# The second norm's shift and scale of layer one: from split weight tiles on TensorE to a weighted sum on VectorE

## What is computed

```python
mod = jax.nn.silu(c) @ w_mod[l] + b_mod[l]                  # latent tokens; the same with c_ctx for context
sh1, sc1, gt1, sh2, sc2, gt2 = jnp.split(mod[:, None, :], 6, axis=-1)
...
y = (g_a * y_a + g_b * y_b + g_c * y_c) @ w_out
x = x + gt1 * y
x = x + gt2 * swiglu(rms_norm(x, g_norm2) * (1 + sc2) + sh2, w_ffn_in, w_ffn_out)
```

## Time and profile before

| | us |
|---|---|
| median of three runs | 2443.31 |
| time of the profiled execution | 2441.43 |
| its span, first to last instruction | 2439.6 |
| TensorE busy | 2357.4 (97%) |
| VectorE busy | 1340.9 (55%) |
| ScalarE busy | 1046.8 (43%) |
| GpSimd busy | 735.0 (30%) |

### The profile page before, as it was taken

How to read it: one execution, slowest core, us unless ns; L and a number is a source line. 1 busy time by engine, 2 the same in 40 slices (tenths; PEclk the granted TensorE clock), 3 DMA queues, 4 the chain that set the end, 5 groups by cost and what they waited for, 6 DMA issues and landing times.

```text
span 2439.6 us, 33714 instructions
## 1 busy us (share of the span) xinstructions
PE 2357.4 (97%) x13224; PEld 2126.8 (87%) x13224; DVE 1340.9 (55%) x2079; ACT 1046.8 (43%) x2079; POOL 735.0 (30%) x545
## 2 busy tenths in 40 slices
PE   7999999989989999999999999999999999999999
PEld 3888999989989989999999997777878887888887
DVE  5666677699953444454443436767888954211111
ACT  4666667642253342212221227666764253422222
POOL 2211112100064524343333333112220054444443
PEclk9999999999999999999999999999999999999999
DMA  6100111022233414433343322111112323233333
GB/s 253 45 22 28 39 35 44 25 94 83 70 100 104 143 44 130 130 112 119 120 134 109 117 77 78 36 35 41 47 38 84 104 87 129 87 100 94 101 95 95
DMA packets 130828, 209.01 MB, mean 86 GB/s; under 512 B 12784, under 2 KB 58096, under 8 KB 130544
## 3 DMA queue, kind: packets, MB, share of 16 engines
q1 hardware_dynamic: 130672, 206.86, 26.7%
HBM read 202.62 MB, written 4.19 MB: 85 GB/s over the span
## 4 chain that ended last, share of the span: by engine, by line
PE 54%; DVE 5%; ACT 3%; issue 1%; DVEq 0%; ACTq 0%
PE acc L648 15%; PE acc L650 15%; PE acc L649 15%; PE aux L648 2%; PE aux L649 2%; PE aux L650 2%; DVE RB L1629 2%; ACT M L1093 1%; PE sco L832 1%; DVE M L1629 1%; PE aux L845 1%; DVE NM L1672 1%; PE sco L800 1%; ACT RB L1093 1%; ACT R L1093 1%
## 5 line engine op out<-in xcount | busy, mean ns | idle before, releaser
L564 POOL TENSOR_TENSOR WLO<-STG,WHI 128x512 fp32r<-128x512 f32 (+2 forms) x532 | 728.1, 1390 | 1687.0 <-ACT WHI L1089 1686.8
L648 PE MATMUL acc<-H,WHI 128*128 128x384 f32 (+2 forms) x1976 | 710.9, 360 | 14.7 <-DVE H L1885 8.6
L650 PE MATMUL acc<-H,WLO 128*128 128x384 f32 (+2 forms) x1976 | 695.6, 352 | 0.0
L649 PE MATMUL acc<-H,WHI 128*128 128x384 f32 (+2 forms) x1976 | 695.5, 352 | 0.0
L1089 ACT ACTIVATE WHI<-STG 128x512 fp32r<-128x512 f32 (+2 forms) x648 | 348.9, 586 | 409.8 <-PE acc L650 362.1
L648 PEld LDWEIGHTS acc<-H,WHI 128*128 128x128 f32 x1976 | 374.5, 190 | 43.6 <-issue 14.0
L650 PEld LDWEIGHTS acc<-H,WLO 128*128 128x128 f32 x1976 | 374.0, 189 | 25.4
L649 PEld LDWEIGHTS acc<-H,WHI 128*128 128x128 f32 x1976 | 374.7, 190 | 24.0
L648 PE MATMUL acc<-RB,WHI 128*128 128x384 f32 (+1 forms) x816 | 288.6, 354 | 3.2 <-DVE RB L1629 1.4
L1629 DVE TENSOR_TENSOR T<-G,acc 128x384 f32<-128x384 f32 (+1 forms) x101 | 60.3, 597 | 413.7 <-PE acc L650 305.7
L650 PE MATMUL acc<-RB,WLO 128*128 128x384 f32 (+1 forms) x816 | 287.6, 352 | 0.0
(11 more groups left out here) (144 smaller groups left out, 2942.9 us busy)
## 6 DMA issues: line engine op xcount, KB each, us to landing
STG<-in_w_fi SPq DMA_DIRECT2D x176, 256.0 KB, 2.7
M<-in_w_mod SPq DMA_DIRECT2D x56, 512.0 KB, 4.7
STG<-in_w_in SPq DMA_DIRECT2D x104, 256.0 KB, 2.6
STG<-in_w_gate SPq DMA_DIRECT2D x96, 256.0 KB, 2.7
STG<-in_w_fo SPq DMA_DIRECT2D x64, 256.0 KB, 2.7
STG<-in_w_br SPq DMA_DIRECT2D x96, 128.0 KB, 2.1
STG<-in_w_mod SPq DMA_DIRECT2D x48, 256.0 KB, 2.7
FIRST<-in_w_mod SPq DMA_DIRECT2D x8, 1024.0 KB, 20.2
```

The lines of the kernel that those rows point to most:

```text
L564: nc.gpsimd.tensor_tensor(WLO[:, s, a:a + w], STG[:, g, a:a + w], WHI[:, s, a:a + w].bitcast(F32), ALU.subtract).then_inc(S("w_split"), 1)
L648: nc.tensor.matmul(dst, lh, rh, start=first, stop=False)
L649: nc.tensor.matmul(dst, lh, rl, start=False, stop=False)
L650: return nc.tensor.matmul(dst, ll, rh, start=False, stop=last)
```

## The change

The eight groups of sh2 and sc2 leave the weight pipeline. SyncE loads the two parts as 16 raw tiles of 512 KB into RB: tiles 0 to 7 (sh2) into three slots in the homes of branch 1, tiles 8 to 15 (sc2) into four slots in homes of the convolution branch, once `merge(2,7)` is done. VectorE weighs them with two instructions per tile (one per condition) behind `merge(2,4)`, `(2,5)`, `(2,6)` and behind the residuals 1 to 5. TensorE sums each part over the partitions ahead of output tiles 3 and 7. The gates (2,1), (2,2), (2,3) now follow each other with the sums of the convolution norm between them, and ScalarE's order is changed with them. In the merge of branches 0 and 1 VectorE's `mod_groups` now comes first in its turn instead of behind taps and `weights_lo`.

```diff
+SOON = [SH2, SC2]
+SOON_SLOTS = [3, 4]
...
 # merge_order, the last branch
-    if l == 0:
-        order += mod + [("gate", 2, 1)] + mod + [("gate", 2, 2)] + mod + [("gate", 2, 3)] + mod
-    else:
-        order += [("gate", 2, j) for j in AHEAD[l]]
-    order += [("gate", 2, 0)]
+    order += [("gate", 2, j) for j in AHEAD[l]] + [("gate", 2, 0)]
     for j in range(KC):
         order += ([("gate", 2, j)] if j and j not in AHEAD[l] else []) + [("branch", 2, j)]
-        order += mod if j and j not in AHEAD[l] else []
...
+        soon = lambda o: SOONB[:, o * 512:o * 512 + D]
+        SOON_RAW = [[soon(o) for o in (18, 20, 22)], [soon(o) for o in (0, 2, 4, 9)]]
+        SOON_SUM = [[soon(6), soon(12)], [soon(15), soon(18)]]
...
 # SyncE
+            def soon_raws(*tiles):
+                for i in tiles:
+                    n, k = divmod(i, KC)
+                    slots = SOON_SLOTS[n]
+                    if k < slots:
+                        sp.wait_ge(S("madd"), madds(0, 1 + n, KC - 1))
+                    else:
+                        sp.wait_ge(S("soon_w"), 2 * (i - slots + 1))
+                    g = SOON[n] * 4
+                    src = w_mod[g:g + 4, k // 4, :, k % 4 * MOD_GROUP:(k % 4 + 1) * MOD_GROUP].rearrange("g p c -> p g c")
+                    sp.dma_start(SOON_RAW[n][k % slots].rearrange("p (g c) -> p g c", g=4), src).then_inc(S(f"soon{n}_{k % slots}"), 16)
...
+                    if l == 0 and kind == "branch" and b == 2:
+                        soon_raws(*{1: (0, 1, 2), 6: (3, 4, 5), 7: (6, 7)}.get(j, ()))
...
                         tile(w_out[l, j * 2 + s], KC * P)
+                        if l == 0:
+                            soon_raws(*{3: (8, 9, 10, 11), 5: (12, 13), 6: (14, 15)}.get(j * 2 + s, ()))
...
 # TensorE
+            def turn_soon(n):
+                pe.wait_ge(S("soon_w"), 2 * KC * (n + 1))
+                if n == 0:
+                    pe.wait_ge(S("mod_sum"), 1 + c.at("turn"))
+                for k in range(KC):
+                    for s in range(2):
+                        mm = nc.tensor.matmul(soon_cols(n)[:, k, s:s + 1], SOON_SUM[n][s][:, k * P:(k + 1) * P], ONES[:, 0:1],
+                                              start=True, stop=True)
+                mm.then_inc(S("soon_full"), 1)
...
-                    mod_groups(l, 1)
-                    gate_tile(l, 2, 1, between=turn_pending)
-                    mod_groups(l, 1)
-                    at["turned", l, "mean"] = c.at("turn")
+                    turn_pending()
+                    at["turned", l, "mean"] = at["turned", l, "root"] = c.at("turn")
+                    gate_tile(l, 2, 1)
                     conv_sums(l, 0)
-                    turn_pending()
-                    at["turned", l, "root"] = c.at("turn")
-                    gate_tile(l, 2, 2, between=lambda: conv_sums(l, 1), where=(1, 0))
-                    mod_groups(l, 1)
-                    gate_tile(l, 2, 3, between=turn_pending)
-                    mod_groups(l, 1)
+                    gate_tile(l, 2, 2)
+                    conv_sums(l, 1)
+                    gate_tile(l, 2, 3)
...
                     branch_tile(l, 2, j, turn_pending)
-                    half(0, j and j not in AHEAD[l])
-                    half(1, j and j not in AHEAD[l])
...
-                for _ in range(2, KC):
+                for j in range(2, KC):
+                    if l == 0 and j in (3, 7):
+                        turn_soon(j // 4)
                     tile(KC, normed, slim)
...
 # ScalarE
-                    mod_group(l)
                     hi()
                     for r in range(len(slim)):
                         gate_ahead(l, 1, r)
-                    mod_group(l)
                     exp_set()
                     for ch in range(CC):
                         conv_square(l, ch)
                     hi()
-                    gate_ahead(l, 2, 0)
+                    for r in range(len(slim)):
+                        gate_ahead(l, 2, r)
                     conv_root(l)
-                    gate_ahead(l, 2, 1)
-                    mod_group(l)
                     conv_out(l, 0)
                     hi()
-                    for r in range(len(slim)):
-                        gate_ahead(l, 3, r)
+                    gate_ahead(l, 3, 0)
                     conv_out(l, 1)
-                    mod_group(l)
+                    gate_ahead(l, 3, 1)
                     conv_out(l, 2)
...
 # VectorE
+            def weigh_soon(i):
+                n, k = divmod(i, KC)
+                slots = SOON_SLOTS[n]
+                dve.wait_ge(S(f"soon{n}_{k % slots}"), 16 * (k // slots) + 16)
+                for u in range(2):
+                    src, dst, gain = SOON_RAW[n][k % slots], SOON_SUM[n][u], SC[:, k, u:u + 1]
+                    if k == 0:
+                        nc.vector.tensor_scalar(dst, src, gain, None, ALU.mult).then_inc(S("soon_w"), 1)
+                    else:
+                        dve.wait_ge(S("soon_w"), 2 * (i - 1) + u + 1)
+                        nc.vector.scalar_tensor_tensor(dst, src, gain, dst, ALU.mult, ALU.add).then_inc(S("soon_w"), 1)
...
                         start, end = merge_tiles(l, b, j)
+                        mod_groups(at["turned", l, b, j])
                         if end - start == 3:
                             weights_lo(start + SLOTS + 1)
                         conv_taps(l, MERGE_TAPS[l][KC * b + j])
                         weights_lo(end + SLOTS)
-                        mod_groups(at["turned", l, b, j])
                         merge(b, j)
...
                     merge(2, j)
+                    for i in {4: (0, 1, 2), 5: (3, 4, 5), 6: (6, 7)}.get(j, ()) if l == 0 else ():
+                        weigh_soon(i)
...
                         add_square(j - 1, n)
+                    if l == 0 and j in (3, 7):
+                        soon_sum(j // 4)
+                    for i in {1: (8, 9), 2: (10, 11), 3: (12,), 4: (13, 14), 5: (15,)}.get(j, ()) if l == 0 else ():
+                        weigh_soon(i)
```

More of the change, by code:

```diff
@@ L142, in merge_order @@
     half = lambda q, here=True: [("mod", q, None)] if l == 0 and here else []
-    mod = half(0) + half(1)
     order = [("gate", 0, j) for j in range(EARLY)]
@@ L213, in build @@
         with nc.sbuf_tensor("FIRST", [P, 2 * MOD_FIRST, KC * P], F32) as FIRST:
+            pass
+        with nc.sbuf_tensor("UNDER", [P, 2 * KC * TOK], F32), nc.sbuf_tensor("SOONB", [P, 2 * KC * TOK], F32) as SOONB:
             pass
@@ L368, in raws_upto, with soon_cols @@
             return max([i for end, i in ends if end + RAW_LAG <= tiles], default=0)
+        def soon_cols(n):
+            return sco[n][:, 512:512 + 2 * KC].rearrange("p (k s) -> p k s", s=2)
         def turned_cols(n):
@@ L720, in branch_tile @@
                      ready=("bsplit", 8 * l + 4 * b) if b < 2 else ("c_split", CC * l), between=between)
[L722 to L725, removed]
             def turn_pending():
@@ L1045, in _ @@
                             if g == 0:
-                                pe.wait_ge(S("mod_sum"), 1 + c.at("turn"))
+                                pe.wait_ge(S("soon_sum"), len(SOON))
                             turn_cols(TURN_UP[g, f])
@@ L1337, in gate_ahead @@
                 evac_gate(l, 2, j, at[(l, 2, j, "gate"), r], ahead_store(l, j, a, w), a, w)
-            def mod_group(l):
-                if l == 0:
-                    hi()
-                    hi()
-                    mod_row()
             def conv_square(l, ch):
@@ L1554, in _ @@
                             merged_hi(l, k)
-                        if l == 0:
-                            mod_row()
-                            hi()
                         merged_hi(l, 5)
                         merged_hi(l, 6)
-                        if l == 0:
-                            hi()
-                    elif l == 0 and j and j not in AHEAD[l]:
-                        hi()
-                        hi()
-                        mod_row()
                 merged_hi(l, KC - 1)
@@ L1848, in weigh_raw, with soon_sum @@
                         nc.vector.scalar_tensor_tensor(dst, src, gain, dst, ALU.mult, ALU.add).then_inc(S("gv"), 1)
+            def weigh_soon(i):
[9 more added lines that the diff above has]
+                        nc.vector.scalar_tensor_tensor(dst, src, gain, dst, ALU.mult, ALU.add).then_inc(S("soon_w"), 1)
+            def soon_sum(n):
+                dve.wait_ge(S("soon_full"), n + 1)
+                bias = V[:, V_BMOD:V_G].rearrange("p (l a k s) -> p l a k s", l=DEPTH, a=6, s=2)[:, 0, SOON[n], :, :]
+                tt(MOD[:, 0, SOON[n], :, :], soon_cols(n), bias, ALU.add).then_inc(S("soon_sum"), 1)
             def col_sum(n):
@@ L1891, in norm @@
                     dve.wait_ge(S("mod_sum"), c.at("mod") + 1)
+                    dve.wait_ge(S("soon_sum"), len(SOON))
                     if l:
```

## The result

The changed kernel takes a median of 2428.01 us in four runs (2426.32 to 2428.85), beside 2443.55 us for the kernel before in four runs: a ratio of 0.9935, interval 0.9923 to 0.9948, some 15.5 us less. That lies in the range of the prediction (2416.5 to 2431.0) and 5.4 us above its number, 2422.6. The profiled execution took 2426.32 us.

What follows compares the result with a forecast made beforehand. TensorE, busy 97% of the span, was taken as the bound, with VectorE setting the pace in branch 0. 18.9 + 8.7 + 0.7 + 1.9 - 7.4 - 1.1 - 1.0 = 20.7 us off 2443.31 gave 2422.6, range 2416.5 to 2431.0.

Steps and rivals of the forecast that it cites:

- Step 1: Between branch tiles (1,7) and (2,0): four gates and two sets of sums remain, 35.8 us instead of 54.7; gain 18.9.
- rival A: Ahead of branch tile (2,0): the convolution's norm becomes the bound, 8.5 us lost plus 1.6 slow clock; 2432.7 us, chance 0.11.
- Step 2: Gates (2,4) to (2,7): turns of 12.45 us instead of 15.33 gain 8.7; the last group gains 0.7.
- Step 3: Output projection: two groups of 32 column instructions cost TensorE 7.4 us, the slow clock behind them 1.1.
- Step 4: VectorE's weighing: hidden in the last branch, costs 1.0 us in the output projection behind residual 4; bounds 0 and 3.
- Rival B: Last branch and output projection: VectorE is overloaded by the weighing, 7 us lost, 2430 us, chance 0.10.
- Step 5: SyncE's load queue: holds for raw tiles cost 0; ScalarE may stand 2.5 us, TensorE not at all.
- rival C: SyncE's load queue: its holds starve TensorE and the kernel gets slower, 2448.5 us, chance 0.03.
- Step 6: Branch 0: with mod_groups first, TensorE enters branch 1 earlier by 1.9 us, had once; bounds 0 and 4.
- D: Whole change: the removed work was filling time everywhere and the gain vanishes, 2443 us, chance 0.02.

Runs made afterwards that it cites:

- x12: Changed kernel with columns spread between products, first part's sums ahead of the output projection, group sums behind the taps, and merge(2,7) before the low parts: 2415.76 us.
- x1: Changed kernel with VectorE's group sums put back behind the taps and low parts: 2425.36 us, ratio 0.9921 to the kernel before.
- x11: Changed kernel with VectorE's group sums put back behind the taps and low parts, run again: 2427.23 us, ratio 0.9940 to the kernel before.

## Why the prediction came out as it did

**Step 1, the four gates: held.** The wait, the transposes and the slow matmuls are gone and nothing new waits; 35.9 us stand where 35.8 were laid out. Measured with undisturbed branch 1, the stretch fell from 154.8 (mean) to 135.4, 19.4 us, where 18.9 were forecast. Reading ScalarE's Silu steps as waits for gates that were not there yet, and not as work, was the point that decided between the forecast and rival A: the chain took 14.1 us, not 25.4. A was close all the same, with 3.0 us of cover.

**Step 2, the turns: held.** 8.5 for 8.7, and 0.6 for 0.7 at the last group, which had only filled VectorE's time. The prediction argued that VectorE's order causes this wait, and x12 shows it.

**Step 3, TensorE's new work: the own time held, the clock term failed.** The two groups last 3.6 us each where nothing else happens. The term behind them was "One in three, twice: 1.1", from the windows of one execution. The rate was luck of that execution. In the three traces of the changed kernel the groups are followed by 6.8, 10.2 and 10.2 us at the lower clock, 3.4 to 5.1 us lost. The timeline of the changed kernel shows the first of them:

```profile
812.47 4.84 PE L817 MATMUL sco<-K,SOONB 128*128 128x1 f32 x32
...
817.64 0.52 PE L671 MATMUL acc<-H,WHI 128*128 128x384 f32 x1
817.96 0.52 PE L672 MATMUL acc<-H,WLO 128*128 128x384 f32 x1
```

Here the clock falls inside the group, which then takes 4.84 us, and the products behind it start 0.32 us apart as in the earlier trace rows. The stretch grew by 12.5 us, where steps 3 and 4 together said 9.5. The bound of 3.4 that the prediction gave was too low as well, since it took one stretch of 3.4 us, 1.7 lost, per group; in two of the three traces 5.1 are lost.

**Step 4, the weighing: the size held.** One wait of 0.8 us, for X at output tile 6, where 1.0 was forecast there. The traces agree with the reading of the two engines' contention: two tiles in a row behind a residual take 6.82 us, as the 7.0 said. The Trainium skill ("SBUF — State Buffer", section Who interferes with whom) puts such contention down to ports that VectorE shares with GpSimd; the row agrees with its size here, and no run took GpSimd's splits away to test the cause. The row in the timeline of the changed kernel, the two tiles and the wait they cause:

```profile
837.71 6.82 DVE L1868 SCALAR_TENSOR_TENSOR SOONB<-SOONB,SC 128x1024 f32<-128x1024 f32 x4
...
845.12 0.44 PE L670 MATMUL acc<-H,WHI 128*128 128x384 f32 x1 [0.76 <-DVE X L1976]
```

Rival B fell: the turns of the last branch last 12.5 us, and six weighings (9.34 us) fit into one beside its merge.

**Step 5, SyncE: held.** TensorE waits for no load in this stretch; rival C fell. ScalarE does, as the prediction allowed. Its copy for gate tile (2,7), the load held behind raw tiles 3 to 5:

```profile
756.83 1.24 ACT L1114 ACTIVATE WHI<-STG 128x512 fp32r<-128x512 f32 x2 [4.92 <-DMA STG<-in_w_gate]
```

The slot was free once branch tile (2,5) had ended, at 754.8, so 2.1 of the 4.92 us are the load's, where 2.5 were allowed. TensorE began the tile at 767.08 without a wait.

**Step 6, the sums first: failed.** "Gain 1.9" took the end of one wait for a gain. VectorE paces branch 0, as the prediction itself said, so TensorE waits for the next thing that VectorE makes. What was left is 0.6 us in branch 0, and the wait's new place puts a stretch at the lower clock into branch 1 in five traces of eight. In the traces it is a loss of 0.8 in the mean, in the medians nothing.

**The sum.** Steps 1 and 2: 28.5 measured, 28.3 forecast. Steps 3 and 4: -12.5 and -9.5. Step 6: -0.8 and +1.9. That is 15.2 against 20.7, and 15.5 in the medians. The gap of the forecast is 3.0 in steps 3 and 4, which is the clock behind the columns, and 2.7 in step 6. Rivals A and D would have given about 11 and 0. The measured 2428.01 stands at the very end of the forecast's own range, 2417 to 2428; the room above it, to 2431.0, was there for rival B, which did not happen. So the range held with little to spare, and both steps that missed, 3 and 6, promised too much gain.

What stays open: why the stretch behind a group is now 3.4 and now 6.8 us long, and why three of the 13 groups in the output projection have none. In x1 and x11, one and the same kernel, the output projection took 90.2 and 86.6 us for that reason.

## What to carry to other kernels

How often a clock falls is a rate: read it from several executions before it goes into a sum, for one trace is one draw, and the difference of two single traces holds microseconds that no edit made. Narrow matmuls in a row cost more than their own time here; put them between wide ones, or into a wait that is there anyway. Where a helper engine sets the pace, a reorder on it moves the wait of the other engine and gains only what it shortens in the helper's own work.

## What the runs showed of the hardware

Behind a group of 32 one-column instructions in a row, 3.6 us in which the profile counts TensorE as busy, the granted clock fell to 0.50 in 38 of 43 groups in the SwiGLU block and between the output tiles. With two of them between every three matmuls of 384 columns it stayed at 1.00 in 17 groups, but for the one stretch named above. The group of 16 in a row near the end of the SwiGLU block (1.8 us) was followed by no fall in any of the ten traces that have it. A column instruction costs 0.11 us in a row and the same between wide products, so the wide ones hide none of it.
